# Prompt attention of a decoder trunk: heads in pairs on two halves of the partitions, two pairs in flight, transposed pieces per bank

## What is computed

```
def sparse_attend(q, ks, vs, idx, pos_q):
    logits = jnp.einsum('nthd,ntkhd->nthk', q, ks).astype(jnp.float32) * ATT_SCALE
    valid = (idx <= pos_q[None, :, None])[:, :, None, :]
    p = jax.nn.softmax(jnp.where(valid, logits, -jnp.inf), axis=-1).astype(q.dtype)
    return jnp.einsum('nthk,ntkhd->nthd', p, vs)
...
        idx = index_select(qib, wib, ki, pos_q, k_sel)
        return sparse_attend(qb, k[nidx, idx], v[nidx, idx], idx, pos_q)
```

## Time and profile before

| | us |
|---|---|
| median of 3 runs | 2984.64 |
| lowest and highest run | 2980.1, 2989.83 |
| the profiled execution | 2987.36 |
| its span, first to last instruction | 2985.3 |
| TensorE busy in the span | 2721.0 (91%) |
| VectorE busy | 1552.2 (52%) |
| ScalarE busy | 874.8 (29%) |
| mean granted clock of TensorE | 0.93 |

### The profile page before, as it was taken

The page is one execution under the profiler, slowest core; times in us unless marked ns, Lnnn a source line. Parts: engine busy times, 40 slices in busy tenths (PEclk is TensorE's granted clock), DMA queues, the critical chain, the costliest instruction groups (busy, mean ns, idle before and its releaser), DMA issues.

```text
span 2985.3 us, 42021 instructions
## 1 busy us (share of the span) xinstructions
PE 2721.0 (91%) x15608; PEld 2488.8 (83%) x15608; DVE 1552.2 (52%) x1858; ACT 874.8 (29%) x1338; POOL 1035.6 (35%) x752
## 2 busy tenths in 40 slices
PE   7899979999999999789985888798799999999995
PEld 7899969999999999686783245568699999999995
DVE  2422366454353452648868986931465551552544
ACT  2211153122121222516611244451342221221223
POOL 2222753433232337517714000004634332333355
PEclk9999979999999999799997955899799999999997
DMA  3111101211111111120113400001112111111111
GB/s 125 35 42 43 44 27 49 66 47 50 57 42 57 49 42 58 52 64 26 62 42 118 127 15 1 1 1 43 35 36 70 46 46 57 49 50 52 47 50 70
DMA packets 65099, 148.53 MB, mean 50 GB/s; under 512 B 6923, under 2 KB 31051, under 8 KB 64747
## 3 DMA queue, kind: packets, MB, share of 16 engines
q1 hardware_dynamic: 57984, 132.29, 14.5%
q10 hardware_dynamic: 7018, 14.99, 1.4%
HBM read 137.15 MB, written 10.11 MB: 49 GB/s over the span
## 4 chain that ended last, share of the span: by engine, by line
PE 78%; issue 8%; DVE 6%; POOL 5%; ACT 2%; DMA 1%; POOLq 1%; SPq 0%; DVEq 0%; ACTq 0%
PE PS L431 22%; PE PS L434 22%; PE PS L432 22%; PE PS L686 2%; PE PS L709 2%; POOL SCT L1221 2%; PE PS L698 1%; POOL WL L1105 1%; DVE SCT L1566 1%; POOL Z L1171 1%; PE PS L643 1%; DVE m8b L1568 1%; PE PS L664 1%; DVE m8a L1568 1%; ACT PR L1048 1%
## 5 line engine op out<-in xcount | busy, mean ns | idle before, releaser
L432 PE MATMUL PS<-XL,WH 128*128 128x352 f32 x3168 | 1028.1, 325 | 0.0
L431 PE MATMUL PS<-XH,WH 128*128 128x352 f32 x2976 | 969.1, 326 | 32.9 <-POOL WL L1105 18.6
L1105 POOL TENSOR_TENSOR WL<-RAW,WH 128x1024 fp32r<-128x1024 f32 x210 | 532.2, 2535 | 1112.0 <-ACT WH L769 1112.0
L434 PE MATMUL PS<-XH,WL 128*128 128x352 f32 x2976 | 648.0, 326 | 0.0
L431 PEld LDWEIGHTS PS<-XH,WH 128*128 128x128 f32 x2976 | 566.3, 190 | 59.7 <-issue 42.0
L432 PEld LDWEIGHTS PS<-XL,WH 128*128 128x128 f32 x3168 | 602.0, 190 | 0.0
L434 PEld LDWEIGHTS PS<-XH,WL 128*128 128x128 f32 x2976 | 515.3, 190 | 0.0
L769 ACT ACTIVATE WH<-RAW 128x1024 fp32r<-128x1024 f32 x210 | 223.4, 1064 | 610.2 <-PE PS L434 588.4
L431 PE MATMUL PS<-HH,WH 128*128 128x352 f32 x1056 | 341.8, 324 | 17.8 <-POOL WL L1105 13.8
L432 PE MATMUL PS<-HL,WH 128*128 128x352 f32 x1056 | 341.2, 324 | 0.0
L1359 DVE SCALAR_TENSOR_TENSOR cv<-ext,fpar,cv 128x1072 f32<-128x1072 f32 x88 | 287.6, 3268 | 12.3 <-DVE cv L1355 0.2
(11 more groups left out here) (249 smaller groups left out, 3481.6 us busy)
## 6 DMA issues: line engine op xcount, KB each, us to landing
RAW<-in_slabs SPq DMA_DIRECT2D x210, 512.0 KB, 3.5
KP<-in_ck SPq DMA_DIRECT2D x32, 256.0 KB, 3.3
VP<-in_cv SPq DMA_DIRECT2D x32, 256.0 KB, 2.9
out_o_y<-Z ACTq DMA_DIRECT2D x6, 704.0 KB, 3.3
Z<-in_xT ACTq DMA_DIRECT2D x4, 528.0 KB, 8.7
Z<-in_xT SPq DMA_DIRECT2D x4, 528.0 KB, 10.5
out_o_k<-K ACTq DMA_DIRECT2D x1, 2112.0 KB, 7.9
kix<-in_kidx SPq DMA_DIRECT2D x32, 64.0 KB, 1.8
```

Of the source, the lines that this page charges most:

```text
L431: pe.matmul(o, WH[j][:, k, :], hi[:, k, c * TW:(c + 1) * TW], start=first, stop=False)
L432: pe.matmul(o, WH[j][:, k, :], lo[:, k, c * TW:(c + 1) * TW], start=False, stop=False)
L434: mm = pe.matmul(bank_set(j)[:, c, :], WL[j][:, k, :], hi[:, k, c * TW:(c + 1) * TW], start=False, stop=last)
L1105: pool.tensor_tensor(WL[j][:, :, :], RAW[j][:, :, :], WH[j][:, :, :].bitcast(F32), ALU.subtract).then_inc(w_lo, 1)
```

## The change

The 64 units become 32 pairs p = 4b + c: heads 2c and 2c + 1 of block b. x is 0 or 1.

- TensorE computes both heads' logits in one step, in alternation for each 512 keys, and both heads' values in one step, in alternation for each key tile.
- Up to pair 15 (`WIDE` = 16) the logits take banks 2(p mod 2) + x, and pair p + 2 is issued ahead. From pair 16 they take banks 0 and 1 for x = 0 and 2 and 3 for x = 1, and pair p + 1 is issued ahead, after both exponentials of pair p.
- The transposed tiles come in pieces of at most four, each with a bank (4 and 5 by turns) and a copy of its own.
- The probabilities and their transposes have four buffers from pair 16, two of them where the rotary tables lay.
- The orders of TensorE, ScalarE and VectorE are written anew, and the search rounds are spread as `[2] * 7 + [3] * 14 + [4] * 2 + [0] * 9` over the pairs.
- ScalarE does the first exponential of the prompt ahead of the last sample's copy to spt.

```
-        PR = [at(f"PR{j}", [P, NP], F32, wh_off + j * 4096) for j in range(2)]
-        PT = [at(f"PT{j}", [P, 8, P], F32, wh_off + (2 + j) * 4096) for j in range(2)]
+        PR = [at(f"PR{j}", [P, NP], F32, o) for j, o in enumerate((wh_off, wh_off + 4096, E0 + 8192, E0 + 12288))]
+        PT = [at(f"PT{j}", [P, 8, P], F32, o) for j, o in enumerate((wh_off + 8192, wh_off + 12288, E0, E0 + 4096))]
...
+        def logits_of(p, x):
+            n = keys_of(p)
+            return PS[:, 2 * (p % 2) + x, 0:n] if p < WIDE else pair(x, n)
...
+        def pieces_of(p, x):
+            i, b = pieces(2 * p + x), p // 4
+            return [(i, range(0, min(4, b + 1)))] + ([(i + 1, range(4, b + 1))] if p >= WIDE else [])
+        def ahead(p):
+            return p + 2 if p + 2 < WIDE else p + 1 if WIDE <= p + 1 < PAIRS else None
...
-        slot_rounds = [6] + [7] * 6 + [6] + [1] * 16 + [1] * 16 + [2] * 16 + [0] * 16
+        slot_rounds = [6] + [7] * 6 + [6] + [2] * 7 + [3] * 14 + [4] * 2 + [0] * 9
...
+            def logits(p):
...
+                if p < 2:
                     pe.wait_ge(sexp, SEQS - 1)
+                    pe.wait_ge(c_kept, 8)
+                elif p < WIDE:
+                    pe.wait_ge(aexp, 2 * (p - 1))
                 else:
+                    pe.wait_ge(aexp, 2 * p)
                 for a in range(0, n, 512):
                     w = min(512, n - a)
+                    for x in range(2):
+                        half = slice(64 * x, 64 * x + 64)
+                        mm = pe.matmul(logits_of(p, x)[:, a:a + w], Q[half, c, b * P:(b + 1) * P], K[half, c, a:a + w],
+                                       start=True, stop=True)
                 mm.then_inc(lg, 1)
+            def turn_probs(p, x):
+                pe.wait_ge(anorm, 2 * p + x + 1)
+                src_ = probs_of(p, x)
+                for i, ts in pieces_of(p, x):
+                    if i >= 2:
+                        pe.wait_ge(ate, i - 1)
+                    for t in ts:
+                        mm = pe.transpose(PS[:, piece_bank(i), (t % 4) * P:(t % 4 + 1) * P], src_[:, t * P:(t + 1) * P],
+                                          ident[:, :])
+                    mm.then_inc(atp, 1)
+            def values(p):
+                b, c = p // 4, p % 4
+                pe.wait_ge(ate, pieces(2 * p + 2))
+                if p >= 2:
+                    pe.wait_ge(ao_lo, p - 1)
                 for t in range(b + 1):
+                    for x in range(2):
+                        o = PS[64 * x:64 * x + 64, 6 + p % 2, 0:P]
+                        h = 2 * c + x
+                        mm = pe.matmul(o, VT[:, t, h * HD:(h + 1) * HD], turned_of(p, x)[:, t, :], start=(t == 0), stop=(t == b))
                 mm.then_inc(apv, 1)
...
+            sample_values_turn(1)
+            pe.wait_ge(ste, 2 * SEQS)
+            pe.wait_ge(satt, 2 * HEADS)
+            pe.wait_ge(sexp, SEQS)
+            for p in range(PAIRS):
+                if ahead(p):
+                    logits(ahead(p))
+                turn_probs(p, 0)
+                turn_probs(p, 1)
+                if p:
+                    values(p - 1)
+            values(PAIRS - 1)
...
+            exp(0, 0)
+            sample_turned(SEQS - 1)
+            exp(0, 1)
+            sample_kept(1)
+            sample_out(1)
+            for x in range(2):
+                exp(1, x)
+            for p in range(2):
+                for x in range(2):
+                    norm_probs(p, x)
+            for p in range(PAIRS):
+                n = ahead(p)
+                for x in range(2):
+                    turned_probs(p, x)
+                    if n:
+                        exp(n, x)
+                if p:
+                    attended(p - 1)
+                if n:
+                    for x in range(2):
+                        norm_probs(n, x)
...
+            for p in range(2):
+                for x in range(2):
+                    row_max(p, x)
+            for p in range(2):
+                for x in range(2):
+                    row_recip(p, x)
+            for p in range(PAIRS):
+                n = ahead(p)
+                if n:
+                    row_max(n, 0)
+                    row_max(n, 1)
+                rounds(SEQS + p, 0)
+                if n:
+                    row_recip(n, 0)
+                    row_recip(n, 1)
+                if p >= 2:
+                    att_rest(p - 2)
+                rounds(SEQS + p, 1)
```

More of the change, by code:

```diff
@@ L337, in added @@
             return 2 * u - sum(c == 0 for _, c, _, _ in UNITS[:u])
[L340 removed]
+        SLOTS = SEQS + PAIRS
         BEST = TOPK_P // 8
@@ L348, in build @@
         assert start_round[SLOTS] == ROUNDS
-        assert all(start_round[SEQS + 8 * blocks[0]] >= 2 * BEST * (g + 1) for g, blocks in enumerate(GROUPS))
+        for p in range(PAIRS):
+            n = ahead(p)
+            if n and n % 8 == 0 and n // 4 in (2, 4, 6):
+                assert start_round[SEQS + p] >= 2 * BEST * (n // 8), (p, n)
         @block.sync
@@ L1044, in norm_probs @@
[L1044 to L1068, removed]
+            def exp(p, x):
+                act.wait_ge(amax, 2 * p + x + 1)
+                if p == 1:
+                    act.wait_ge(sv_turned, 2)
+                elif p == WIDE:
+                    act.wait_ge(atp, pieces(2 * (p - 1 + x)))
+                elif p >= 2:
+                    act.wait_ge(atp, pieces(2 * (p - 2) + x + 1))
+                act.activation(probs_of(p, x), logits_of(p, x), ACT.Exp, scale=-1.0, bias=small_of(nmx, p, x),
+                               accum_out=small_of(psm, p, x)).then_inc(aexp, 1)
@@ L1069, in _, with attended @@
+            def attended(p):
+                b, c = p // 4, p % 4
+                act.wait_ge(apv, p + 1)
+                act.activation(ZR[:, 4 + c, b * P:(b + 1) * P], PS[:, 6 + p % 2, 0:P], ACT.Copy).then_inc(ao_hi, 1)
+            for k in range(SEQS):
                 if k >= 1:
-                    sample_turned(k - 1) if k <= SEQS else turned_probs(k - 1 - SEQS)
-                if k < SLOTS:
-                    sample_exp(k) if k < SEQS else exp(k - SEQS)
+                    sample_turned(k - 1)
+                sample_exp(k)
@@ L1086, in _ @@
+            attended(PAIRS - 1)
+            act.wait_ge(atp, pieces(2 * PAIRS))
             split_high(OUT1)
```

137 lines of the change are left out of this document (67 added, 70 removed).

## The result

The changed kernel took 2929.69 us, median of 4 runs (2928.88 to 2935.2), against 2984.93 for the kernel before (4 runs): ratio 0.9823, 95% interval 0.9808 to 0.9839. Faster by 55 us, where 48 were forecast. The profiled execution took 2930.36 us with a span of 2928.6, so 57.0 us less than the one profiled before.

What follows compares the result with a forecast made beforehand. Two bounds were seen to alternate: TensorE doing heads one by one, and VectorE's 179 us of work. Gains of 22.7 and 26.0 us gave 2938.7, or 2935.9 by the median; forecast 2937, range 2923 to 2967.

Steps and rivals of the forecast that it cites:

- The start: After the first row maxima, the last sample's copy waits behind the first prompt exponential; VectorE was to idle 10.7 us.
- Blocks 0 to 5: Prompt attention's first part: VectorE works without a gap after the start, reaching unit 48's row maximum at 1913.3; gain 22.7 us.
- VectorE's sum: Blocks 0 to 5: VectorE's 179.4 us of busy time, taken over unchanged, plus 10.7 us idle.
- the sum: Whole kernel: gains of 22.7 and 26.0 make 48.7 us, giving 2938.7 from the profiled execution or 2935.9 by the median.
- Blocks 6 and 7: Prompt attention's last part, without search rounds: 59.4 us against 85.4, a gain of 26.0 us.
- The rings: Blocks 6 and 7: logits, first transposes, then copies and exponentials twice, through one buffer; 6.3 and 6.9 us a pair.
- the term for the slow ring: Entering blocks 6 and 7, TensorE is still at 1.2 GHz; 2.3 us added for most of one ring.
- The row of 32-partition outputs: Trace evidence for overlapping values: four samples' eight passes of 512 took 1.09 us, one sample's eight 3.62.
- the rival of serial values: Blocks 4 to 7: two heads' values run in sequence, logits side by side; 2950 us, chance 0.12.
- The rival of 1.2 GHz for the last eight pairs: Blocks 6 and 7: TensorE's clock stays low, rings of 10.2 and 11.5 us; 31 more, 2968 us, chance 0.13.
- the coarse row: Profile's coarse clock row, read as showing TensorE's clock low in just the slices of the prompt attention.
- the two terms of the stage: Prompt attention: gains of 22.7 us in blocks 0 to 5 and 26.0 us in blocks 6 and 7.

## Why the prediction was right, and where it was off

*The start* was right. The copy came where it was put, the sample values started 1.1 us after the first row maximum, not 1.3, eight passes took 6.05 and not 5.5, and VectorE idled 10.6 us for 10.7. That this came so close is partly luck: sample values and tail took 7.1 us for 6.5, and the steps behind them to the reciprocal 3.5 for 4.3. That ScalarE's order causes 7 us of it is shown by the kernel with the copy first.

*Blocks 0 to 5*: the mechanism (VectorE without a gap behind the start) is shown by its waits, and by both spreads of the rounds. The mis-sized term is VectorE's sum: "1723.2 + 179.4 + 10.7" took the busy time of before as fixed, and the changed kernel needs 175.57 for the same rounds and row maxima. By form, of before and then of after (instructions, busy us, mean ns):

```profile
L1684 DVE RECIPROCAL prc<-psm 128x1 f32<-128x1 f32 x48 | 7.5, 156 | 26.5 <-ACT PR L1041 26.2
L1678 DVE CUSTOM_DVE_ANT_0 PS<-PS,SCT 128x768 f32<-128x768 f32 x8 | 7.6, 956 | 0.0
L1695 DVE TENSOR_TENSOR XL<-PS,ZR 128x128 fp32r<-128x128 f32 x23 | 6.3, 272 | 0.0
```

```profile
L1744 DVE RECIPROCAL prc<-psm 128x1 f32<-128x1 f32 x48 | 5.3, 150 | 10.5 <-ACT PR L1086 10.5
L1739 DVE CUSTOM_DVE_ANT_0 PS<-PS,SCT 128x768 f32<-128x768 f32 x8 | 7.5, 982 | 0.0
L1755 DVE TENSOR_TENSOR XL<-PS,ZR 128x128 fp32r<-128x128 f32 x21 | 5.8, 276 | 0.0
```

48 reciprocals of the same 0.15 us cover 2.2 us less, since two of a pair now follow each other and overlap; the row maxima of all six lengths sum to 28.9 us instead of 30.0 in the same way, and two rests fall behind the mark (0.5). That is 3.8 us less, the size by which the sum was off, though the rounds' groups took 0.8 more, so as much stays open. The stretch ended 4.0 us earlier after its start than forecast: 186.1 for 190.1, a gain of 26.7 and not 22.7.

*Blocks 6 and 7*: 58.4 for 59.4. The rings, from logits to logits, are as forecast but for the first, whose logits ran at a granted 0.52 (1.00 from their end on):

```profile
1911.45 3.26 PE L724 MATMUL PS<-K,Q 64*128 64x512 f32 x8 [4.63 <-ACT PR L1086]
1919.36 1.77 PE L724 MATMUL PS<-K,Q 64*128 64x512 f32 x8 [0.72 <-ACT PR L1086]
1925.63 1.77 PE L724 MATMUL PS<-K,Q 64*128 64x512 f32 x8 [0.50 <-ACT PR L1086]
1931.91 1.99 PE L724 MATMUL PS<-K,Q 64*128 64x512 f32 x8 [0.50 <-ACT PR L1086]
```

The first took 7.91 us where 6.3 and 2.3 were allowed, the next two 6.27 and 6.28 for 6.3. Three rings of block 7, to the logits at 1952.44, took 20.53 for 20.7, and what follows 13.29 for 13.4. So 0.7 of the 1.0 us is the term for the slow ring, which cost 1.6 and not 2.3. That the copies and exponentials are parts of the ring is shown by the kernel with the exponentials together. Logits of a pair as those of one head was right; values, put at one head's plus 10%, came out at one head's, 1.97 for 1.96; they lie beside the ring.

The row of 32-partition outputs was the right one to go by, and the Trainium skill's rule ("TensorE: Matmul & The Clock Gate", "Part 3: Packing small matmuls — row/col tiling": a weight load overlaps matmuls in flight only when the row group differs) is not borne out here: the 32 passes, each with its own load on all rows, take 0.062 us apiece when the heads alternate, against 0.1225 for one head alone, and the 32 loads lie beside the matmuls (1949.87, 1.73 us long). The same section of the Trainium skill also lets a load for the background weight buffer run ahead of the matmuls; no run here tells whether that is what happens. With 1.97 us for the 32 passes the rival of serial values fell. Its price had been put at 13 us (7 in the rings, 3.8 at the end, 2 in blocks 4 and 5). The kernel with the values apart lost 6.0: 2.6 between the first row maximum of block 6 and that of pair 31, 3.4 behind it, and nothing in blocks 0 to 5. It is not quite that rival, since its values take 3.33 and not 3.8.

The rival of 1.2 GHz for the last eight pairs fell: a granted 0.97 there, with mainly the first logits (3.26 us for 1.77) slow. In blocks 0 to 5 the clock did not rise with the pairs, 0.67 for 0.66. Behind the start that cost nothing, since TensorE was busy 62% of the stretch and VectorE waited 0.5 us beside the gap. One reading of the coarse row was too strong: the clock is also at 0.7 in five slices outside the stage, and only the two slices at 0.5 are its own.

The 3.4 us of the profile that lie outside the stage had no term in the sum; against the medians, 55.2 us, it is 1.6 us. So of the 7.3 us by which 2937 was too high, 4.9 are the two terms of the stage (53.6 for 48.7), 1.1 is the step from 2935.9 to 2937, and 1.3 lie outside the stage or in the medians.

## What to carry to other kernels

Cost a stretch by the engine that has the most work left once the change is made, not by the one that leads the chain of waits today: here taking a third off TensorE's busy time in blocks 0 to 5 was worth no more than VectorE's sum allowed. What remained (10 us at the start, copies inside a ring, six half steps of the search moved to block 6) was worth another 20. When an engine becomes the bound, look for work that it can do later in a stretch where it waits, and for the order of two steps on another engine that opens a gap in it. Busy time isn't conserved when the order changes: the 48 reciprocals, of 0.15 us each, covered 7.5 us one by one and 5.3 in pairs.

## What the runs showed of the hardware

Matmuls on two halves of the output columns (or of the contraction rows) run side by side without standing next to each other in the program. For the 32 value passes of a pair turns of two and of four passes take 1.97 and 2.02 us, of eight 2.57, of sixteen 3.33. In the last two, some three passes of 0.109 us are hidden at each change of head: the other half's first pass starts while three of the first half's are still to come. Four passes of 512 columns ahead of four of the other half lose nothing (1.99 us). What holds the passes that are still to come was not tried.
